# The begin of layer 1 in a hybrid-layer kernel: three latent chunks side by side, and layer outputs moved behind them on ScalarE

## The reference, cut to what matters

```
for l in range(2):
    u = x * (1.0 + scale) + shift
    proj = u @ w_in            # 1024 x ...: q_lat 384, kv_lat 256, k_rope 32 and others
    q  = rms_norm(q_lat, q_norm_g) @ w_uq     # 8 heads, 64 + 32 each
    kv = rms_norm(kv_lat, kv_norm_g) @ w_ukv
    ...                        # attention, two convolution branches, a gated merge
    x = layer_norm(ALPHA * x + gate * out, ln_g, ln_b)
```

## Time and profile before

| | us |
|---|---|
| median of 3 runs | 2220.85 (2219.37 to 2221.35) |
| the profiled execution's own time | 2220.64 |
| its span, first to last instruction | 2218.9 |

### The profile page before, as it was taken

One profiled execution on the slowest core, in us unless ns is written; L12 is line 12 of the kernel. 1 busy time (PEld: TensorE's weight loads), 2 busy tenths in 40 slices (PEclk: granted clock), 3 DMA queues, 4 the chain that ended last, 5 costly groups with the idle time before them and its releaser, 6 DMA issues.

```text
span 2218.9 us, 31199 instructions
## 1 busy us (share of the span) xinstructions
PE 2163.9 (98%) x11368; PEld 1757.6 (79%) x11368; DVE 1424.1 (64%) x2306; ACT 873.9 (39%) x1470; POOL 1076.0 (48%) x1269
## 2 busy tenths in 40 slices
PE   8999999999999999999999999999999999999998
PEld 6777778888687777888677888887787887788886
DVE  3698858763568886987677565628576776533322
ACT  3644453222654445222353333334344344433321
POOL 3555437665355544776435443332434344344443
PEclk9999999999999999999999999999999999999999
DMA  8222227753322223765323222232424232222222
GB/s 287 88 88 84 76 82 259 247 200 115 104 95 86 77 76 111 235 208 186 105 67 108 100 92 89 93 116 100 133 69 152 96 123 91 67 76 76 77 77 76
DMA packets 97829, 259.93 MB, mean 117 GB/s; under 512 B 10638, under 2 KB 20238, under 8 KB 97564
## 3 DMA queue, kind: packets, MB, share of 16 engines
q1 hardware_dynamic: 76224, 212.51, 29.7%
q10 hardware_dynamic: 21468, 45.56, 5.7%
HBM read 237.01 MB, written 20.97 MB: 116 GB/s over the span
## 4 chain that ended last, share of the span: by engine, by line
PE 70%; issue 14%; POOL 8%; DVE 5%; ACT 2%; DMA 1%; ACTq 0%; POOLq 0%; DVEq 0%
PE bank L2250 21%; PE bank L2252 21%; PE bank L2251 21%; POOL t L493 7%; DVE t L1907 2%; PE bank L2501 2%; PE bank L2514 1%; PE bank L2525 1%; PE bank L2350 1%; DVE t L1359 1%; DMA t<-w_ada 1%; PE bank L2669 0%; DVE t L1865 0%; DVE t L1355 0%; PE bank L2366 0%
## 5 line engine op out<-in xcount | busy, mean ns | idle before, releaser
L493 POOL TENSOR_TENSOR t<-t,t 128x256 fp32r<-128x256 f32 x1168 | 995.7, 885 | 972.0 <-ACT t L586 971.7
L2250 PE MATMUL bank<-t,t 128*128 128x512 f32 x3012 | 1155.8, 384 | 13.8 <-DVE t L1355 6.0
L2251 PE MATMUL bank<-t,t 128*128 128x512 f32 x3012 | 1127.6, 374 | 0.0
L2252 PE MATMUL bank<-t,t 128*128 128x512 f32 x3012 | 1127.1, 374 | 0.0
L2250 PEld LDWEIGHTS bank<-t,t 128*128 128x128 f32 x3012 | 567.1, 188 | 142.4 <-issue 10.2
L2251 PEld LDWEIGHTS bank<-t,t 128*128 128x128 f32 x3012 | 567.4, 188 | 103.2 <-issue 4.3
L2252 PEld LDWEIGHTS bank<-t,t 128*128 128x128 f32 x3012 | 566.3, 188 | 104.3
L586 ACT ACTIVATE t<-t 128x1024 fp32r<-128x1024 f32 x302 | 317.2, 1054 | 294.9 <-PE bank L2252 261.7
L1701 DVE SCALAR_TENSOR_TENSOR t<-t,t,t 128x512 f32<-128x512 f32 x240 | 217.4, 906 | 7.7 <-ACT t L775 1.0
L1421 DVE SCALAR_TENSOR_TENSOR t<-t,t,t 128x512 f32<-128x512 f32 x168 | 160.9, 978 | 37.7 <-ACT t L872 25.4
L1359 DVE SCALAR_TENSOR_TENSOR t<-t,bank 128x512 f32<-128x512 f32 x112 | 76.7, 685 | 127.7 <-ACT t L1299 57.6
(11 more groups left out here) (277 smaller groups left out, 1669.9 us busy)
## 6 DMA issues: line engine op xcount, KB each, us to landing
t<-blocks SPq DMA_DIRECT2D x306, 512.0 KB, 3.6
t<-w_ada SPq DMA_DIRECT2D x160, 256.0 KB, 4.2
t<-w_ada SPq DMA_DIRECT2D x14, 512.0 KB, 10.1
xm_park<-t ACTq DMA_DIRECT2D x16, 384.0 KB, 2.3
s_park<-t ACTq DMA_DIRECT2D x16, 384.0 KB, 2.3
t<-xm_park ACTq DMA_DIRECT2D x16, 384.0 KB, 4.7
t<-s_park ACTq DMA_DIRECT2D x16, 384.0 KB, 5.4
xc_park<-t ACTq DMA_DIRECT2D x16, 256.0 KB, 2.0
```

The lines of the kernel that those rows point to most:

```text
L493: low = pool.tensor_tensor(w_lo[slot][:, part], w_raw[slot][:, part], w_hi[slot][:, part].bitcast(F32), ALU.subtract)
L2250: pe.matmul(out, wh, xh, start=start, stop=False)
L2251: pe.matmul(out, wh, xl, start=False, stop=False)
L2252: return pe.matmul(out, wl, xh, start=False, stop=stop)
```

## The change

TensorE: in layer 1, `first_chunks` takes the three q_lat chunks together (9 matmuls a tile) and the `u_chunk` of q_lat 2 goes. Ahead of kv_lat 1, whose bank is also the one that `x_norm` reads, stands a wait for the last `x_norm`. ScalarE: the three q_lat chunks are copied out without splits between them, their squares follow at once, and the next two blocks (90 and 91) are split after the squares. The eight layer outputs move behind the root for q and the splits of blocks 92 and 93. The stores of `x` are issued later: three ahead of the root for kv, the other five each behind one of the first five query heads.

```diff
-def park_layer(l):
+def park_layer(l, js):
     act.wait_ge(act_done, A(l, "y", KT - 1))
-    for j in range(KT):
+    for j in js:
         act.dma_start(x_park[j], x[:, j, :]).then_inc(x_parked, 16)
...
 for j in range(3):
-    made_ahead = l and j == 1
-    evac(q_lat[:, j, :], banks[(0, 1, 4)[j]][:], (l, "q_lat", j), B_QL(l) + j if l and j != 1 else None)
-    if made_ahead:
-        for i in range(KT):
-            layer_out(l - 1, i)
-        split_to(B_QL(l) + j + 1 + RING)
+    evac(q_lat[:, j, :], banks[(0, 1, 4)[j]][:], (l, "q_lat", j), None)
...
 for j in range(3):
     square(tmp[U_TMP[j]][:], q_lat[:, j, :], "q_lat", j, None)
 if l:
-    evac(kv_lat[:, 0, :], banks[3][:], (l, "kv_lat", 0), B_KVL(l))
+    split_to(B_QL(l) + 2 + RING)
+    evac(kv_lat[:, 0, :], banks[3][:], (l, "kv_lat", 0), None)
...
 act.activation(tmp[2][:, 0:128], banks[2][:, 0:128], ACT.Sqrt, ...)      # q_std
 if l:
-    park_layer(l - 1)
+    split_to(B_KVL(l) + 1 + RING)
+    for i in range(KT):
+        layer_out(l - 1, i)
 evac(kv_lat[:, 1, :], banks[6][:], (l, "kv_lat", 1), None)
...
 split_to(B_KVL(l) + 2 + RING)
+if l:
+    park_layer(l - 1, range(3))
 act.wait_ge(pe_done, P(l, "kv_sq", 1))
...
     evac(qf[0:NOPE, h, :], banks[Q_BANK[h % 4]][0:NOPE, :], (l, "q", h), None)
+    if l and h < KT - 3:
+        park_layer(l - 1, (3 + h,))
...
 # TensorE
-    first_chunks(banks[0:2], B_QL(l), [(l, "q_lat", j) for j in range(2)], lambda k: Dn(l, "uL", k))
-    u_chunk(banks[4], B_QL(l) + 2, (l, "q_lat", 2))
+    first_chunks((banks[0], banks[1], banks[4]), B_QL(l), [(l, "q_lat", j) for j in range(3)], lambda k: Dn(l, "uL", k))
     u_chunk(banks[3], B_KVL(l), (l, "kv_lat", 0))
...
 if l:
+    pe.wait_ge(dve_done, Dn(l - 1, "x_norm", KT - 1))
     u_chunk(banks[6], B_KVL(l) + 1, (l, "kv_lat", 1), turn)
```

## The result

The changed kernel takes 2229.69 us (median of 6, 2227.2 to 2231.31) against 2220.96 for the kernel before measured beside it, a ratio of 1.0039 (95% interval 1.0029 to 1.0049). It is slower by 8.7 us. Its profiled execution took 2230.91 us, with a span of 2228.5 us.

What follows compares the result with a forecast made beforehand. TensorE, busy 98% of the span, was taken to bound the kernel. Stall 6.4 + clock 1.7 + 0 = +8.1 us on the profiled 2220.64 gives 2228.7, predicted median 2228.9; range 2225.5 to 2232.5.

Steps and rivals of the forecast that it cites:

- Nothing to win in the stretch: Layer 1 start to kv_lat 0: TensorE already streams unbroken at 0.227 us a step; reordering ScalarE could return at most 0.6 us.
- The stall, 6.4 us: Ahead of kv_lat 0, TensorE waits from 585.09 to 591.4 for block 90's low part; first step 0.1 longer.
- The cheapest order: Copy of q_lat 0, then block 90's split at once: low part at 588.3, against 591.4 in the diff's order.
- What had hidden the wait: Before kv_lat 0: q_lat 2's 24 matmuls (5.4 us) and a slot freed while they ran; both covers go together.
- The clock, 1.7 us: Behind the pause TensorE runs at half speed for three microseconds and somewhat more, losing 1.7 us; ends 0 and 3.4.
- Three chunks, x_norm: Taking three q_lat chunks together, and waiting for the last x_norm ahead of kv_lat 1, each cost nothing.
- ScalarE's later part: From the sums of squares to the root for kv: copy of kv_lat 1 0.3 us late but hidden; cost 0.
- S: Start of the sums of squares on TensorE, 590.62 in the kernel before; later ScalarE times are counted from it.
- the tight place: Block 97: GpSimd ends at 620.16, TensorE wants it at 620.6; store delay beyond 0.4 us shows; expected 0, upper end 0.5.
- The stores: Eight issues on ScalarE's queue run beside its backlog; expected cost 0, upper end about 1 us at the root for kv.
- The ends of the range: 2225.5: stall alone 1.4 us cheaper, pauses won back; 2232.5: upper ends of the clock and the stores.
- Stall alone: Rival, chance 0.2: the 6.4 us wait ahead of kv_lat 0 without a loss of clock, giving 2227.3 us.

Runs made afterwards that it cites:

- Own slot: The changed kernel with separate high and low buffers for block 90 and its split ahead of the eight uH; ratio 0.9997, median 2220.83 us.
- split before squares: The changed kernel with block 90's split right behind the copy of q_lat 0, ahead of the other copies and the squares; ratio 1.0018, median 2225.25 us.
- outputs first: The changed kernel with the eight layer outputs put between the squares and the split of block 90; ratio 1.0059, median 2233.93 us.
- Pair again: The changed kernel with TensorE's order undone, q_lat 0 and 1 as a pair, then q_lat 2; ScalarE keeps the new order; ratio 1.0037, median 2229.67 us.
- stores together: The changed kernel with all eight stores issued together right behind the layer outputs and none later; ratio 1.0065, median 2235.48 us.
- filled wait: The changed kernel with six unused matmuls of ones between the q_lat chunks and kv_lat 0; ratio 1.0029, median 2228.15 us.
- pair and early splits: The changed kernel with TensorE's order undone and blocks 90 and 91 split early again; layer outputs and stores stay late; ratio 0.9999, median 2220.41 us.

## Why the prediction was right

The time was forecast as 2228.9 and is 2229.69. The stall and the clock behind it came where they were put, and nothing else was added. One sentence on what had hidden the wait before is not borne out.

- **Nothing to win in the stretch.** Right. The two kernels without the pause, one of them with all of the change in it, measure 0.9999 and 0.9997. The short slower steps, which bounded the gain at 0.6 us, did not move. The timeline of the kernel before has three more of 0.1 us in kv_lat 1, at 591.75, 594.38 and 595.72, so the bound was nearer 0.9.
- **The stall, 6.4 us.** Measured 6.20 and 0.1 for the start behind it. The chain through copy, squares, split and low part came as worked out, a tenth or two shorter in sum. Own slot, split before squares and outputs first set this term to 0, 3.3 and 11.1 us, and the time went with it each time. The cheapest order was priced at 588.3 for the low part, a pause of 3.2; split before squares shows 3.28.
- **What had hidden the wait.** Wrong in part. The prediction names two covers that go together: the 24 matmuls of q_lat 2, and a slot that comes free while they run. Pair again gives both back and has the same pause of 6.19 us. The cover was the place of the split, right behind the copy of q_lat 0 (579.66 in the earlier trace rows). The changed kernel loses it twice, by ScalarE's order and by the slot, and either is enough for a pause: 6.2 us by the order, about 2.8 by the slot (an estimate: 3.28 less the 0.5 of the copy).
- **The clock, 1.7 us.** The mechanism is right, the size was too small: 2.4 us in the profile of the changed kernel, and 1.4, 1.7, 2.0 and 2.1 behind the first pause of pair again, split before squares, outputs first and stores together. I took half of a stretch somewhat over three microseconds; the clock was at half for 5 us of work. With 2.4 in place of 1.7 the sum is 2229.6.
- **Three chunks, x_norm.** Cost 0, as the own slot shows for the chunks. No wait for x_norm appears in the profile; no run takes that wait out.
- **ScalarE's later part.** The root for q came at S + 0.9 (600.54), as forecast, the copy of kv_lat 1 at S + 8.0 (forecast 8.1), the root for kv at S + 13.2 (612.77), as before. At the tight place, GpSimd ends block 97 at 629.15 and TensorE wants it at 629.62, 0.5 us ahead as before.
- **The stores.** Cost 0 in these places is right, and shown by the run with pair and early splits. The reason given, that issues run beside the engine's backlog, holds only where there is a backlog. Stores together had none, and eight issues cost about 6 us.
- **The ends of the range.** They don't quite follow from the terms: 2228.9 + 1.7 + 1.5 makes 2232.1 where 2232.5 stands, and 2227.3 - 1.4 - 0.6 makes 2225.3 where 2225.5 stands. Nothing hangs on it.
- **What it rested on in luck.** Stall alone and forecast lie 1.7 us apart, less than single runs of one kernel spread. The medians alone could not have told them apart; the seam of the filled wait did. That the clock would cost 1.7 rather than 1.4 or 2.4 could not be known from the one row that there was.

## What to carry to other kernels

In a ring of three slots, a step that feeds the next block depends on who frees the slot and on what the feeding engine does ahead of it; write both down before reordering either. Work that is late for nobody should go behind the feeding step, and work that is needed soon is still wrong ahead of it, if another engine is waiting for the feed. On an engine whose queue also issues DMAs, spread the issues or put them where the engine has work left; behind a wait for its own last result they stand alone.

## What the runs showed of the hardware that was not expected

The same pause of 6.2 us cost 2.4 us of half clock in one profile and 1.4 in another, and 11.1 us of pause cost 2.0: the loss did not grow with the pause. What it goes by is how long TensorE works at 0.50 behind the pause. First the fall and the return of the clock in the changed kernel, then in pair again:

```profile
589.00:590.00 1.00, 0.00 (x0) 0.00 (x0) 0.00 (x0) 0.64 (x1) 1.00 (x2) 0.93 0.00 0
596.00:597.00 1.00, 1.00 (x4) 0.82 (x3) 0.00 (x0) 0.00 (x0) 0.00 (x0) 0.66 0.91 360
```

```profile
589.00:590.00 1.00, 0.00 (x0) 0.00 (x0) 0.00 (x0) 1.00 (x3) 0.00 (x0) 0.51 0.00 0
595.00:596.00 1.00, 1.00 (x4) 0.77 (x4) 0.00 (x0) 0.00 (x0) 0.57 (x1) 0.57 0.70 283
```

Worked out from these shares, the clock is at half from 589.9 to 596.7 in the first and from 589.0 to 595.9 in the second. TensorE resumes at 591.60 and at 592.87, and so works at half for 5.1 and for 3.0 us. A step takes 0.427 us there instead of 0.227, which makes 2.4 and 1.4 us. The fall came 4.3 us behind the end of the last matmul of q_lat in the one and 2.2 us in the other; why is not shown.

Behind a pause of 3.28 us, TensorE resumed at 1.00 and fell to half about 1.5 us later, in the middle of dense matmuls. The kernel before shows the same near its begin: TensorE resumes at 15.38, the window 15 to 16 still stands at 0.90, and only 16 to 19 at 0.50.

An issue of a 256 KB store took ScalarE's queue 619 ns in the median when eight were issued close together, 5.33 / 8 = 0.67 us in the run with all stores at once, and 330 ns in the median when five of eight stood two microseconds or more apart.
